# A second expert step with fixed experts, loaded ahead of the ranking, and another opening order

## The reference, cut to what matters

```
x <- x + gate1(c) * W_out( sig(g_hy) * P_hy(Hyena(h)) + sig(g_at) * P_at(DilatedAttn(h)) )
x <- x + gate2(c) * GroupedMoE(adaLN(RMSNorm(x), c))
```

```
scores = sigmoid(t @ router_w)                  # 16 experts in 4 groups
idx    = top 2 experts of the best group        # per token
gates  = scores[idx] / sum(scores[idx])
y      = sum over e of gates[:, e] * ((silu(t @ w1[e]) * (t @ w3[e])) @ w2[e])
```

## Time and profile before

| | us |
|---|---|
| median of 3 runs | 1157.45 (1154.95 to 1157.7) |
| the profiled execution, own time | 1153.2 |
| its span | 1151.3 |
| PE busy | 1058.8 |
| DVE busy | 468.1 |
| ACT busy | 164.7 |
| moved by DMA | 334.86 MB, mean 291 GB/s |

### The profile page before, as it was taken

The page is one execution under the profiler, slowest core; times in us unless marked ns, Lnnn a source line. Parts: engine busy times, 40 slices in busy tenths (PEclk is TensorE's granted clock), DMA queues, the critical chain, the costliest instruction groups (busy, mean ns, idle before and its releaser), DMA issues.

```text
span 1151.3 us, 17534 instructions
## 1 busy us (share of the span) xinstructions
PE 1058.8 (92%) x7487; PEld 581.3 (50%) x7487; DVE 468.1 (41%) x1022; ACT 164.7 (14%) x322; POOL 17.3 (2%) x35
## 2 busy tenths in 40 slices
PE   4899999999997999997979999999999799998785
PEld 2578766755444444432428876675444444433231
DVE  3367798551026222351225678930102612222103
ACT  2021100220014111110121110022001411101002
POOL 3000000000000000000000000000000000000000
PEclk9899988999998999999999999899999899999898
DMA  9997846547663999999999874542443499999993
GB/s 312 391 339 266 293 147 221 184 146 257 223 232 124 384 417 419 415 415 419 416 397 334 292 273 167 202 169 70 163 165 147 186 419 416 419 415 417 416 417 130
DMA packets 99282, 334.86 MB, mean 291 GB/s; under 512 B 4810, under 2 KB 5159, under 8 KB 82689
## 3 DMA queue, kind: packets, MB, share of 16 engines
q1 hardware_dynamic: 96093, 323.55, 72.8%
q0 software_dynamic: 2224, 8.17, 1.9%
q10 hardware_dynamic: 884, 1.97, 0.5%
HBM read 332.63 MB, written 1.05 MB: 290 GB/s over the span
## 4 chain that ended last, share of the span: by engine, by line
PE 79%; DMA 9%; DVE 5%; SPq 4%; issue 1%; ACT 1%; DVEq 0%; ACTq 0%
PE bank L681 76%; DMA ring<-in_moe_w_dram 9%; SPq L615 3%; PE bank L926 1%; PE bank L729 1%; PE bank L1084 0%; PE bank L830 0%; DVE area L1548 0%; DVE area L1546 0%; PE bank L1007 0%; DVE hT L1892 0%; ACT L1335 0%; DMA stat<-in_hf_freq_dram 0%; PE bank L997 0%; PE bank L1087 0%
## 5 line engine op out<-in xcount | busy, mean ns | idle before, releaser
L681 PE MATMUL bank<-ring,hT 128*32 128x512 f32 (+3 forms) x2128 | 347.6, 574 | 31.2 <-DMA ring<-in_moe_w_dram 24.8
L681 PEld LDWEIGHTS bank<-ring,hT 128*32 128x32 f32 (+2 forms) x2128 | 141.3, 134 | 213.3 <-issue 209.3
L681 PE MATMUL bank<-hT,ring 128*32 128x256 f32 (+1 forms) x2112 | 216.8, 388 | 1.6 <-DVE hT L1508 1.6
L681 PEld LDWEIGHTS bank<-hT,ring 128*32 128x32 f32 (+1 forms) x2112 | 159.5, 135 | 57.3 <-issue 11.0
L681 PE MATMUL bank<-ring,area 128*32 128x512 f32 x896 | 99.2, 594 | 1.3 <-ACT area L1357 0.9
L1927 DVE TENSOR_TENSOR area<-bank,area 128x512 f32<-128x512 f32 x14 | 9.7, 692 | 189.9 <-PE bank L681 189.9
L681 PE MATMUL bank<-area 32*64 32x64 f32 (+4 forms) x560 | 74.5, 327 | 0.0
L681 PEld LDWEIGHTS bank<-area 32*64 32x64 f32 (+3 forms) x560 | 38.5, 150 | 47.8 <-issue 46.5
L681 PEld LDWEIGHTS bank<-ring,area 128*32 128x32 f32 x896 | 27.7, 110 | 62.9 <-issue 60.3
L681 PE MATMUL bank<-ring,wide 128*128 128x512 f32 x128 | 56.4, 596 | 0.0
L681 PE MATMUL bank<-area,xn 128*128 128x128 f32 x448 | 56.1, 287 | 0.1
(11 more groups left out here) (258 smaller groups left out, 807.5 us busy)
## 6 DMA issues: line engine op xcount, KB each, us to landing
ring<-in_moe_w_dram SPq DMA_DIRECT2D x174, 1024.0 KB, 16.2
ring<-in_w_in_dram SPq DMA_DIRECT2D x26, 2048.0 KB, 11.4
ring<-in_w_ada_dram SPq DMA_DIRECT2D x24, 2048.0 KB, 9.1
wide<-in_moe_w_dram SPq DMA_DIRECT2D x18, 1024.0 KB, 19.5
ring<-in_w_out_dram SPq DMA_DIRECT2D x4, 2048.0 KB, 8.0
ring<-in_w_br_h_dram SPq DMA_DIRECT2D x4, 1536.0 KB, 7.9
ring<-in_w_br_a_dram SPq DMA_DIRECT2D x2, 1024.0 KB, 4.9
area<-in_decay_dram POOLq DMA_DIRECT2D x2, 768.0 KB, 14.2
```

The source lines that it names most:

```text
L681: return pe.matmul(dst, lhsT, rhs, start=start, stop=stop, skip_group_check=True)
```

## The change

- The second expert step is fixed as well, to experts 1 and 14 with 64 places each; twelve experts are ranked, in five steps, of which two have three experts. Their transfers need no ranking, and SP waits for it at step 2.
- In layer 0 one block (w1 of expert 1), in layer 1 two blocks (w1 of experts 1 and 14) go into extra slots in the filters' memory, and are issued before the step 0 blocks are all issued, or right after. The extra slots stay in use for some steps (`EXTRA_LAST`).
- w2 is read by rows: a partition gets four consecutive rows instead of four that lie 128 apart, so that half a block is one run of 8 KB per partition, as for w1 and w3, instead of two of 4 KB. The transposes of the product read with a stride of four to match.
- DVE makes `rows_to_h` of step 0 ahead of the ranking.
- Head of layer 0: `ada(0)` goes before the taps; four taps stay ahead of the first chunk and four go behind chunks 0 and 1; the butterflies go to chunks 2 and 3, the spectra to chunks 5 to 8, `ada(2)` ahead of the wait for the vectors, three `ada_post` one or two chunks later.
- `conv_back` does the one-row matmul and the one beside it in a single matmul of 258 columns.

```
-FIRST = (0, NE - 1)
+FIXED = ((0, NE - 1), (1, NE - 2))
+FIRST = FIXED[0]
...
-PLAN = (((0, 3), (13, 1)), ((1, 3), (12, 1)), ((2, 2), (8, 1), (9, 1)), ((4, 2), (5, 2)),
-        ((3, 2), (10, 1), (11, 1)), ((6, 2), (7, 2)))
+PLAN = (((0, 3), (11, 1)), ((1, 3), (10, 1)), ((2, 2), (8, 1), (9, 1)), ((3, 2), (6, 1), (7, 1)), ((4, 2), (5, 2)))
...
-FILTER_C = 2
+FILTER_C = 5
-EXTRA_LAST = 3
+EXTRA_LAST = {(0, 0): 3, (0, 1): 0, (1, 0): STEPS, (1, 1): 3}
+AHEAD = [[(1, 0, 0)], [(1, 0, 0), (1, 0, 1)]]
...
+        def moe(L):
+            first = [key for key in MOE if key[0] == 0]
+            rest = [key for key in MOE if key[0] and key not in AHEAD[L]]
+            return first[:4] + AHEAD[L][:1] + first[4:] + AHEAD[L][1:] + rest
...
-                if (L, kind) == (DEPTH - 1, "moe") and b == (1, 0, 0):
-                    free.extendleft(((RING + 1, None), (RING, None)))
+                if kind == "moe" and b in AHEAD[L]:
+                    free.appendleft((RING + b[2], None))
                 r, old = free.popleft()
-                while r == RING + 1 and b[0] > EXTRA_LAST:
+                while r >= RING and b[0] > EXTRA_LAST[L, r - RING]:
                     r, old = free.popleft()
...
                 elif r == RING:
-                    sp.wait_ge(p_br, (L + 1) * 8)
+                    sp.wait_ge(p_br, L * 8 + 4)
...
-                        if s == 1:
+                        if s == len(FIXED):
                             sp.wait_ge(v_order, L + 1)
...
-                    name, order = (...)[m], "(k p) f -> p k f" if m == 2 else "(p k) f -> p k f"
+                    name, order = (...)[m], "(p k) f -> p k f"
...
-                    for u in range(8):
-                        taps(u, 0)
                     ada(0)
+                    taps(0, 0)
+                    taps(1, 0)
                     ada(1)
+                    taps(2, 0)
+                    taps(3, 0)
...
+                    for u in taps_after(L, c):
+                        taps(u, L)
                     for u in spectra_after(L, c):
                         spectrum(u, L)
-                    if c in (7, 11, 15):
-                        ada_post(4 + (c - 7) // 4)
+                    if c in (9, 13, 16):
+                        ada_post(4 + (c - 8) // 4)
...
-                    even, odd = bank[c % 4][:, 0:FOLD], bank[c % 4][:, SEQ:SEQ + FOLD]
-                    mm(even, Kr[:, 0, part], ictab[:, 0, :], True, False)
-                    mm(even, Ks[:, 1, part], istab[:, 1, :], False, False)
-                    mm(even, Ks[0:1, 0, part], nyquist, False, True)
-                    mm(odd, Ks[:, 0, part], istab[:, 0, :], True, False)
+                    even, odd = bank[c % 4][:, 0:FOLD], bank[c % 4][:, FOLD:2 * FOLD]
+                    mm(bank[c % 4][:, 0:2 * FOLD], Ks[:, 0, part], istab_both, True, False)
+                    mm(even, Kr[:, 0, part], ictab[:, 0, :], False, False)
+                    mm(even, Ks[:, 1, part], istab[:, 1, :], False, True)
                     last = mm(odd, Kr[:, 1, part], ictab[:, 1, :], False, True)
...
-                        last = pe.transpose(bank[0][:, f * P:(f + 1) * P], act[:, f * P:(f + 1) * P], ident)
+                        last = pe.transpose(bank[0][:, f * P:(f + 1) * P], act[:, f::NF], ident)
...
-                    if L == 0 and c < 2:
-                        butterfly(0, c)
+                    for u in taps_after(L, c):
+                        decayed(u, L)
+                    if L == 0 and c in (2, 3):
+                        butterfly(0, c - 2)
```

More of the change, by code:

```diff
@@ L516, in trunk_kernel @@
                 loads.append((L, kind, b, None))
-            elif b[2] == 0:
-                loads += [(L, kind, b[0:2] + (e,), h) for h in range(2) for e in range(max(TILES[b[0]]) + 1)]
+            elif b in AHEAD[L]:
+                loads += [(L, kind, b, h) for h in range(2)]
+            else:
+                together = [(L, kind, b[0:2] + (e,)) for e in range(max(TILES[b[0]]) + 1) if b[0:2] + (e,) not in AHEAD[L]]
+                if b == together[0][2]:
+                    loads += [key + (h,) for h in range(2) for key in together]
         def released(L, kind, b, half):
@@ L549, in spectra_after, with taps_after @@
             return range(u, u + 2) if L == 0 and c >= FILTER_C and u < 8 else ()
+        def taps_after(L, c):
+            return range(4 + 2 * c, 6 + 2 * c) if L == 0 and c < 2 else ()
         def nyquist_after(L, c):
@@ L785, in _ @@
                     ada_post(1)
-                    ada(2)
                     transposes_to_h()
@@ L1570, in _ @@
                     angle(2)
-                    for u in range(8):
-                        decayed(u, 0)
                     ada_copy(0)
+                    decayed(0, 0)
+                    decayed(1, 0)
                     ada_copy(1)
+                    decayed(2, 0)
+                    decayed(3, 0)
                     dv.wait_ge(p_vec, 1)
@@ L1829, in _, with select, rows_to_h, accumulate @@
                 dv.wait_ge(v_sel, L * STEPS + 1)
-                dv.tensor_tensor(halves(selg[0]), halves(sel), first_two(gate_), ALU.mult)
+                link(dv.tensor_tensor(halves(selg[0]), halves(sel), first_two(gate_), ALU.mult))
+                def select(s):
+                    b = s % 2
+                    for tt in range(NT):
+                        dv.tensor_scalar(selg[b][:, tt, :], iota, where[:, s, tt:tt + 1], token[:, 2, tt:tt + 1],
+                                         ALU.is_equal, ALU.mult)
+                        last = dv.tensor_scalar(selh[:, tt, :], iota, where[:, s, NT + tt:NT + tt + 1],
+                                                token[:, 3, tt:tt + 1], ALU.is_equal, ALU.mult)
+                    link(last)
+                    link(dv.tensor_tensor(selg[b], selg[b], selh, ALU.add))
+                    dv.tensor_scalar(sel, selg[b], 0.0, None, ALU.is_gt).then_inc(v_sel, 1)
+                def rows_to_h():
+                    for k in range(4, ND):
+                        last = dv.tensor_scalar(hg[:, k, :], bank[3][:, (k - 4) * P:(k - 3) * P], A2[:, k:k + 1],
+                                                modT[:, 3 * ND + k:3 * ND + k + 1], ALU.mult, ALU.add)
+                    return last
+                def accumulate(s):
+                    n = L * STEPS + s
+                    k = 0
+                    for tt in range(NT):
+                        for h in range(2):
+                            cols = slice(h * W, (h + 1) * W)
+                            dv.wait_ge(p_sc, n * 4 + k + 1)
+                            if n:
+                                dv.wait_ge(v_acc, (n - 1) * 4 + k + 1)
+                            k += 1
+                            dv.tensor_tensor(x[:, tt, cols], x[:, tt, cols], bank[2 + 2 * tt + h][:, :], ALU.add)\
+                              .then_inc(v_acc, 1)
+                dv.wait_ge(p_hg, L * STEPS * 2 + 2)
+                rows_to_h().then_inc(v_hg, 1)
                 link(dv.tensor_scalar(rt[pos_], rt[pos_], 1.0, None, ALU.subtract))
```

89 lines of the change are left out of this document (32 added, 57 removed).

## The result

The changed kernel takes 1146.51 us (median of 4 runs, 1145.73 to 1147.99) beside 1156.2 for the kernel before (4 runs, 1153.38 to 1157.7) on the same chip: ratio 0.9921, 95% interval 0.9897 to 0.9945. By the ratio that is 9.1 us less where 7.1 were forecast (the interval is 6.4 to 11.9), and 1146.5 lies in the range of 1142 to 1157.5. The profiled execution took 1147.99 around a span of 1146.2.

A forecast was written before the change was run, and what follows sets the result against it. PE was taken to bound the layer heads and DMA the expert stages. The terms -2.5 (head), -5.5 (convolution), +0.5 and +0.4 (expert stages) sum to -7.1 us: 1146.1 profiled, 1150.3 for the median, range 1142 to 1157.5.

The forecast's parts named there:

- the hole: Expert stages: DMA dry for 7.8 us in layer 0, some 23 to 25 us after the first up product in both layers.
- Expert stages, +0.5 and +0.4: Layers 0 and 1, first up product to last w3 wait: 211.8 against 211.3 us and 205.8 against 205.4, slightly longer.
- the account behind it: Expert stages: load times at full DMA rate plus 3.4 us for landing give the last w3 wait, in both layers.
- the preload pays in full: Rival, expert stages: no slot holds the loads, 7.3 and 7.4 us gained, 1134.7 us in all; chance 0.10.
- Convolution, -5.5: Convolution's way back, twelve times: merging the one-row matmul saves some 0.46 us each; bounds 0 and -9.
- all on PE's path, since PE waits for no one there: Convolution's way back: the whole 5.5 us saved on PE was taken to shorten the kernel.
- VectorE's work sets the pace: Convolution's way back: one case of the bound of 0 us gained, with DVE's work on each channel setting the pace.
- The one-row pair: Rival, convolution: the one-row pair costs what others do, so 0 gained there, 1155.8 us in all; chance 0.13.
- Head of layer 0, -2.5: New opening: first chunk at 46.7 instead of 50.36, 0.8 us wait for the second butterfly; bounds -4 and +1.
- w2, at 2.49 us a load: Expert stages: w2 loads take 2.49 us like w1 and w3; bound 2.56 as before, +3.0 us in all.
- rows_to_h and VectorE's slack: Start of expert stages: layer 0's 1.04 us wait for rows_to_h goes; the later ranking leaves DVE 2.7 us of slack.
- The rival on the other side: DVE becomes the bound of step 0, between rows_to_h and the product; at 9 us late 1162.9 us; chance 0.06.

The follow-up runs named there:

- e1: Changed kernel with the extra slots put behind step 0's w2 blocks (layer 1: behind the second preloaded block) in the reuse order; 1143.09 us, ratio 0.9891.
- e2: Changed kernel with no block loaded ahead, step 1 still fixed, layer 1's extra slots joining as before the change; 1144.93 us, ratio 0.9891.
- e10: Changed kernel with extra slots behind w2 in reuse order, second_shift_and_scale first, and three-expert steps at 3 and 6; 1127.44 us, ratio 0.9742.
- e11: Same three edits to the changed kernel as e10, but with no block loaded ahead; 1127.02 us, ratio 0.975.
- e3: Changed kernel with VectorE's second_shift_and_scale put ahead of the seven partial sums of the ada blocks; 1140.96 us, ratio 0.9856.
- e9: Kernel of e3 with the convolution's old way back (five matmuls, one of one row); 1151.26 us, ratio 0.9963.
- e4: Changed kernel with the convolution's old way back (five matmuls, one of one row), VectorE's queue as changed; 1151.33 us, ratio 0.995.

## Why the prediction was right

The forecast was right in sign, in size within 2 us and in the mechanism of the hole. Its steps fared unequally, and that the sum came out is in part luck. The convolution gave 2.0 or 3.4 us net where 5.5 were forecast. The opening, by the second product for the spectrum of layer 0, which starts at 153.46 us before and at 152.00 and 150.00 in the two profiles after, gave 1.5 or 3.5 where 2.5 were forecast. Another 1.7 or 2.1 us came in layer 1 ahead of its spectrum, where the change only moves three column sums. The forecast had nothing there, and what the profiles show beside it is the clock: 0.88 granted in 605 to 625 us before, 0.95 and 0.99 after.

**Expert stages, +0.5 and +0.4: right, with one reason wrong.** The hole came where it was put, to 0.2 us, and for the reason given, the order of reuse of the slots (e1 removes it). T0 to the last w3 wait is 0.45 longer and the same. But the account behind it, that DMA decides the end and each dry microsecond counts, is true of layer 1 only. In layer 0 it closed on the kernel before, and I took that for proof; it closed there because the lead of DMA was just not limited by the slots. The dent of 405 in the GB/s line of the changed kernel (341 in 480 to 485 us) is that limit, touched; the line before has no dent. The rival "the preload pays in full" was therefore mis-sized: 7.3 us in layer 0 were never to be had with steps of three experts at 4 and 5. e1 and e2 show it, e10 and e11 show what lifts it.

**Convolution, -5.5: the instruction was sized right, its place wrong.** No load of one row is left, and each way saves 0.40 at full clock (forecast 0.43). In the kernel before part of them ran at 1.2 GHz, so more was gained up to the sum of the shift than the half of 5.5 that was forecast for a layer: 9.9 us in layer 0, 1.45 of them brought along. The step that failed is "all on PE's path, since PE waits for no one there". Behind the ways stands a sum that needs VectorE, whose queue had 5.1 us of other work ahead of it; the bound "VectorE's work sets the pace" was written down and not followed. The waits took back 5.7 us, and the clock after them 2.5 and 1.5 more (32 matmuls in 9.63 and 8.63 us against 7.15). So the term that the forecast had at 5.5 was 2.0 in this profile and 3.4 in the second, and the 10 us of e3 against e9 are what it is worth where the assumption holds.

**The one-row pair.** The rule of the Trainium skill, TensorE: Matmul & The Clock Gate, section LDWEIGHTS, that a load takes time by its columns, would have made the edit worth nothing. For the loads themselves the trace nearly agrees: at 1.2 GHz one of one row took 0.25 us and one of 128 rows 0.22. The cost is in the gaps of 0.23 us on both sides of the one-row pair, of which the rule says nothing. By the rows a way goes from 1.55 to 1.155 us at full clock, and e9 against e3 says 10.3 us in time. The measurement decides.

**Head of layer 0, -2.5: too small, and not one number.** First chunk at 44.5 instead of the forecast 46.7, since the chain at full clock was shorter than the old one that I carried over, and in the first profile it then waited 2.01 us for w_in, a limit I had not set. The wait before the spectra was 0.47 us for a forecast of 0.8. No wait shows at the moved column sums, as said. T0 came 3.1 and 4.8 us earlier in two profiles, by opening and convolution together, where 5.2 were forecast (2.5 and half of 5.5); in layer 1, 2.5 and 4.1 for a forecast of 2.7.

**w2, at 2.49 us a load: right.** 423 GB/s against 408, 2.1 to 3.4 us by the stages where the bound said 3.0, with layer 0's part unclear. The strided transposes take 284 ns in the mean against 275, near enough to nothing. The rule of the Trainium skill, DMA: Bandwidth & Descriptors, section Specifications (512 B or more for line rate), would have had them alike; no run agrees with it.

**rows_to_h and VectorE's slack: right.** No wait for it after the change, 0.73 and 0.65 us when put back, and PE's wait for the product is 0.88 us as before. The rival on the other side did not come near.

## What to carry to other kernels

When a ring of slots feeds an engine, follow two things through the stage before pricing a preload: which block each slot holds when its turn comes, and whether loading gets so far ahead that all slots are full. A lead that is lost at two places shows as a gain only when both are mended. When one engine gets faster, look for the next thing that it needs from another one and at what stands ahead of that in the other's queue; an edit that looked like 5 us was worth 2 to 5 with a queue in the wrong order and 10 with it in the right one.

## What the runs showed of the hardware that I had not expected

Small faults cost twice through the clock: after a wait of 3.70 us PE took 9.63 us for work of 7.15, and with the wait gone it took 7.15. It doesn't always come so. Over all profiles the 32 matmuls took 9.55 to 9.99 us after eleven waits of 3.63 to 3.70 us, but after five waits of 1.94 to 2.02 us they took 7.15 three times and 8.53 and 8.63 the other two. The same code reached its first chunk in 44.5 us or in 50.5, and the runs of the kernel before spread over 10 us, from 1149.8 at a mean granted clock of 0.971 to 1160.2 at 0.962. All twelve runs with the shift first and the old way back (e9) had 0.959 to 0.964, all five with the merged one (e3) 0.967 to 0.974. That is no clean divide: one of e4's eight runs, with the old way back, had 0.969, and one of e10's six, with the merged one, 0.965; what in the matmul of one row goes with the lower clock is open, and it was not tried by itself.
